# Moving steps of the first block between engines' queues: weight halves, rope-row transposes, a convolution and a gate scan

## The reference, cut to what matters

```python
hx = modulate(rmsnorm(x, norm1_w), sh1, sc1)
hc = modulate(rmsnorm(ctx, norm1_w), csh1, csc1)
aq, ak, av, mq, mk, mv, mo, gates = split(h @ w_in)       # for hx and for hc
aq, ak = rope(rmsnorm(aq)), rope(rmsnorm(ak))             # "rows" below
mq, mk = split(silu(short_conv(concat([mq, mk], -1), conv_qk)))
att = latent_attention(aq, ak, av, cak, cav, sink)        # 4 blocks of 128 queries x 8 heads = 32 units
...
b = jnp.cumsum(lf, -1)                                    # gates, per chunk of 128 tokens
m_t = jnp.maximum(inter, d.max(-1))
```

## Time and profile before

| | |
|---|---|
| median of 3 runs | 2391.23 us (2391.07 to 2391.9) |
| the profiled execution | 2391.57 us |
| its span | 2389.7 us |
| PE busy | 2251.6 us, 94% |
| DVE busy | 1234.8 us, 52% |
| ACT busy | 852.1 us, 36% |
| POOL busy | 363.9 us, 15% |

### The profile page before, as it was taken

The page is one execution under the profiler, slowest core; times in us unless marked ns, Lnnn a source line. Parts: engine busy times, 40 slices in busy tenths (PEclk is TensorE's granted clock), DMA queues, the critical chain, the costliest instruction groups (busy, mean ns, idle before and its releaser), DMA issues.

```text
span 2389.7 us, 28697 instructions
## 1 busy us (share of the span) xinstructions
PE 2251.6 (94%) x11081; PEld 1709.2 (72%) x11081; DVE 1234.8 (52%) x2315; ACT 852.1 (36%) x1498; POOL 363.9 (15%) x273
## 2 busy tenths in 40 slices
PE   7898988779879999999999999999999999999999
PEld 4685677655424676777888888886767788888887
DVE  4643455642102686667654434448776755543442
ACT  4433442432100445544342313334464334322231
POOL 0110123000000454432000000025533200000000
PEclk9999999999999999999999999999999999999999
DMA  8115410258999322221223333232222212333322
GB/s 297 56 46 197 139 36 11 97 186 321 363 387 337 100 71 71 62 79 54 80 89 98 97 97 97 90 92 71 81 61 71 71 58 84 106 99 97 97 87 80
DMA packets 198285, 281.48 MB, mean 118 GB/s; under 512 B 13278, under 2 KB 125448, under 8 KB 198152
## 3 DMA queue, kind: packets, MB, share of 16 engines
q1 hardware_dynamic: 197584, 278.47, 35.0%
q10 hardware_dynamic: 568, 1.19, 0.1%
HBM read 277.52 MB, written 2.10 MB: 117 GB/s over the span
## 4 chain that ended last, share of the span: by engine, by line
PE 76%; DVE 12%; DMA 5%; ACT 4%; issue 2%; SPq 1%; POOL 0%; DVEq 0%; ACTq 0%
PE PS L643 20%; PE PS L645 19%; PE PS L644 19%; PE PS L1401 3%; PE PS L2360 3%; PE PS L2400 2%; PE PS L1383 2%; DMA RX<-in_w_up_dram 1%; PE PS L2267 1%; DVE AL L846 1%; DMA RAW<-in_w_up_dram 1%; PE PS L1393 1%; PE PS L2416 1%; DVE AL L825 1%; DVE AL L838 1%
## 5 line engine op out<-in xcount | busy, mean ns | idle before, releaser
L643 PE MATMUL PS<-OPH,WHI 128*128 128x512 f32 x1224 | 498.3, 407 | 8.2 <-DVE OPL L1440 3.1
L645 PE MATMUL PS<-OPH,WLO 128*128 128x512 f32 x1224 | 481.5, 393 | 0.0
L644 PE MATMUL PS<-OPL,WHI 128*128 128x512 f32 x1224 | 480.5, 393 | 0.0
L594 ACT ACTIVATE WHI<-RAW 128x1024 fp32r<-128x1024 f32 (+2 forms) x286 | 295.5, 1037 | 470.7 <-PE PS L645 461.8
L631 POOL TENSOR_TENSOR WLO<-RAW,WHI 128x1024 fp32r<-128x1024 f32 (+1 forms) x107 | 255.8, 2394 | 1326.8 <-ACT WHI L594 1323.4
L615 DVE TENSOR_TENSOR WLO<-RAW,WHI 128x1024 fp32r<-128x1024 f32 x179 | 214.4, 1200 | 378.4 <-ACT WHI L594 378.4
L643 PEld LDWEIGHTS PS<-OPH,WHI 128*128 128x128 f32 x1224 | 231.9, 189 | 74.5 <-issue 22.5
L645 PEld LDWEIGHTS PS<-OPH,WLO 128*128 128x128 f32 x1224 | 231.8, 189 | 50.0
L644 PEld LDWEIGHTS PS<-OPL,WHI 128*128 128x128 f32 x1224 | 232.3, 190 | 43.6 <-issue 1.0
L643 PE MATMUL PS<-WHI,OPH 128*128 128x512 f32 (+2 forms) x576 | 231.4, 402 | 8.9 <-ACT AL L780 3.8
L645 PE MATMUL PS<-WHI,OPL 128*128 128x512 f32 (+2 forms) x576 | 218.0, 378 | 0.0
(11 more groups left out here) (431 smaller groups left out, 3283.6 us busy)
## 6 DMA issues: line engine op xcount, KB each, us to landing
RAW<-in_w_in_dram SPq DMA_DIRECT2D x102, 512.0 KB, 3.6
RAW<-in_w_ffn_in_dram SPq DMA_DIRECT2D x88, 512.0 KB, 3.5
RX<-in_w_gate_dram SPq DMA_DIRECT2D x42, 512.0 KB, 7.2
RX<-in_w_down_dram SPq DMA_DIRECT2D x42, 512.0 KB, 11.4
RAW<-in_w_ffn_out_dram SPq DMA_DIRECT2D x40, 512.0 KB, 3.4
RAW<-in_w_mod_dram SPq DMA_DIRECT2D x36, 512.0 KB, 4.5
RX<-in_w_up_dram SPq DMA_DIRECT2D x32, 512.0 KB, 10.0
RAW<-in_w_up_dram SPq DMA_DIRECT2D x25, 512.0 KB, 9.2
```

The lines of the kernel that those rows point to most:

```text
L594: hi.up(A.e.activation(q.fhi, q.flat, ACT.Copy), ("w", q.i))
L643: T.e.matmul(o, a[0], b[0], start=first, stop=False)
L644: T.e.matmul(o, a[0], b[1], start=False, stop=False)
L645: return T.e.matmul(o, a[1], b[0], start=False, stop=last)
```

## The change

1. Two pieces' halves (mv's third and fourth) are made between the rope steps of the q rows, on ScalarE and VectorE, in place of behind them.
2. Rows 0 and 1 are turned after mv's third piece, rows 2 and 3 after kv's first; the counter of banks is set back by two so that mk uses the same banks as before.
3. In the attention stage ScalarE's first part of the convolution stands ahead of a weight half (and of the wait for its load) in the same step, its SiLU one step later; VectorE's parts of the convolution are done at steps 7, 9, 15, 16 in place of 6, 8, 14, 16.
4. In steps 32 to 35 VectorE does no step of the gate scan; what is left follows the loop.

```diff
@@ -1180,6 +1180,10 @@
+        def turned0(n):
+            return (0, 0, 2, 2)[n]
@@ pe_proj1
-                    lambda n: pe_rope_turns(min(2 * n, 4)))
+                    lambda n: pe_rope_turns(turned0(n)))
             pe_rows("kv", J["kv"], lhs1, range(6), 256, nothing,
-                    lambda t: [(row_a, (rope_no["kv", t], "q")), (copy_a, ("va", t))], lambda t: None)
+                    lambda t: [(row_a, (rope_no["kv", t], "q")), (copy_a, ("va", t))], lambda t: None,
+                    lambda n: pe_rope_turns(4 if n == 0 else 0))
+            B.i -= 2
@@ act_proj1 (dve_proj1 likewise, with dve_lo and rope_copies(V, "v", ...))
                 if t:
                     act_rope_root(r - 1)
+                if t in (1, 2):
+                    act_hi(J["mv"][t + 1] + 1)
             act_rope_root(3)
             for n, i in enumerate(J["mv"]):
-                act_hi(i + 3)
-                rope_copies(A, "a", min(2 * n, 4))
+                if n >= 2:
+                    act_hi(i + 3)
+                rope_copies(A, "a", turned0(n))
...
-            for i in J["kv"]:
+            for n, i in enumerate(J["kv"]):
                 act_hi(i + 3)
+                rope_copies(A, "a", 4 if n == 0 else 0)
@@ act_between1
             for y in range(34):
+                if y in (6, 8, 14, 16):
+                    act_conv("mq", (6, 8, 14, 16).index(y))
                 if y in HALVES1:
...
-                if y in (6, 8, 14, 16):
-                    act_conv("mq", (6, 8, 14, 16).index(y))
-                if y in (9, 17):
-                    for m in (0, 1) if y == 9 else (2, 3):
+                if y in (10, 18):
+                    for m in (0, 1) if y == 10 else (2, 3):
                         act_conv_end("mq", m)
@@ dve_between1
-                if y in (6, 8, 14, 16):
-                    dve_conv("mq", (6, 8, 14, 16).index(y))
+                if y in (7, 9, 15, 16):
+                    dve_conv("mq", (7, 9, 15, 16).index(y))
@@ dve_att1
-                next(gates, None)
+                if s < 32:
+                    next(gates, None)
```

More of the change, by code:

```diff
@@ L1301, in dve_proj1 @@
                     dve_rope_end(r - 1)
+                if t in (1, 2):
+                    dve_lo(J["mv"][t + 1] + 1)
             dve_rope_end(3)
@@ L1305, in dve_proj1 @@
             for n, i in enumerate(J["mv"]):
-                dve_lo(i + 3)
-                rope_copies(V, "v", min(2 * n, 4))
+                if n >= 2:
+                    dve_lo(i + 3)
+                rope_copies(V, "v", turned0(n))
             for t in range(6):
@@ L1312, in dve_proj1 @@
                     copy_v.up(V.e.tensor_copy(dst[:, :, 0:128], ps(PB["mv", t]).rearrange("p (h e) -> p h e", h=4)), ("mv", t))
-            for i in J["kv"]:
+            for n, i in enumerate(J["kv"]):
                 dve_lo(i + 3)
+                rope_copies(V, "v", 4 if n == 0 else 0)
             for t in range(6):
```

## The result

| | before | after |
|---|---|---|
| median | 2390.85 us (10 runs) | 2383.97 us (10 runs, 2373.13 to 2387.59) |
| profiled execution | 2391.57 us | 2387.59 us |
| its span | 2389.7 us | 2385.8 us |
| mean granted clock of its span | 0.985 | 0.981 |

The account below looks back on a forecast made before the run. TensorE was taken as busy nearly everywhere, so only its waits and lower-clock stretches could yield. Terms 9.9 + 4.1 - 0.5 + 5.1 - 1.9 + 0.8 = 17.5 us gave 2373.7 us, range 2368.5 to 2381.

Parts of the forecast that it names:

- Projection: Projection's mv stage: earlier halves and later-turned rows let TensorE go straight on; gain 9.9 us, bounds 8.0 to 10.5.
- Steps 7 and 8: Attention: unit 8's scores stop waiting for the load; a 1.9 us wait replaces 3.03; gain 4.1 us, 1.9 if clock drops.
- Step 10: Attention: the second convolution stands one step nearer to its user; cost 0 to 1.5 us, taken as 0.5.
- Steps 14 to 16: Attention: unit 15's minimum no longer behind the half; new wait 1.8 us; gain 5.1 us, 3.9 if clock drops.
- Step 18: SiLU one step later: VectorE's gate step meets GpSimd's low half, 2.4 us late, less 0.5 saved; loss 1.9 us.
- Rival A: No collision of gate step and GpSimd's low half at step 18: 2.4 us less, 2371.3 us; chance 0.22.
- Gates held back: Attention's end: TensorE gains 2.2 us, waits 3.8 at the next product, slow matmuls lose 1.4; gain 0.8, between 0 and 2.7.
- a reciprocal under a GpSimd product: Attention's end: reciprocal L1628 taken as not caught by GpSimd's half; if caught, that part's gain is 0 instead of 0.8.
- The sum: Whole kernel: the terms give 17.5 us, and the shift passes unchanged through all later work.
- Rival B: Attention: the new 1.8 to 1.9 us waits drop the clock too; up to 5.4 us, 2377 to 2379; chance 0.20.

Follow-up runs that it names:

- e1: Parts 1 and 2 of the change alone, on the kernel before: 2378.59 us, ratio 0.9954.
- e0_after: The changed kernel unchanged, run a second time: 2383.48 us, ratio 0.9971 to the kernel before.
- e17: The changed kernel with VectorE's sum and products of modulation columns and step 18's gate step moved to step 17: 2375.42 us, ratio 0.9943.
- e16: e7 with VectorE's sum and products of modulation columns and step 18's gate step moved to step 17: 2374.01 us, ratio 0.9932.
- e7: The changed kernel with added matmuls in three TensorE waits (steps 8, 16, first product behind the attention): 2377.94 us, ratio 0.9946.
- e10: e7 with the second SiLU back at step 17: 2373.6 us, ratio 0.9931.
- e15: e14 with VectorE's sum and products of modulation columns and step 18's gate step moved to step 17: 2387.12 us, ratio 0.9992.
- e14: The kernel before with added matmuls ahead of unit 8's scores and step 15's transposes: 2394.21 us, ratio 1.001.
- e12: The kernel before with the second SiLU at step 18 in place of 17, nothing else: 2401.5 us, ratio 1.004.
- e3: Part 4 of the change alone (no gate step in steps 32 to 35), on the kernel before: 2397.2 us, ratio 1.0031.
- e9: The changed kernel with the second SiLU back at step 17: 2380.65 us, ratio 0.9962.
- e8: e1 with added matmuls ahead of unit 8's scores and step 15's transposes: 2378.34 us, ratio 0.9951.

## Why the prediction was wrong, step by step

**Projection: right.** 9.9 forecast, 9.8 in both traces of the changed kernel and in e1's. The part seems to bring more where the clock stays up behind the 2.5 us wait that follows (1.6 us in e1's trace), a gain that the forecast did not have.

**Steps 7 and 8: mechanism and wait right, clock half right.** Forecast 4.1, or 1.9 with a drop. Measured at unit 9: 3.7 without a drop (e0_after), 2.4 and 1.0 with one (after, e17). I took the two waits of the earlier trace rows, 1.92 us with no slow matmul behind it and 2.49 with one, for a boundary. It isn't one: two traces with the same 2.08 us wait fall on either side, and behind the very wait of 2.5 us e1's clock stayed up.

**Step 10: right.** 0.5 forecast, 0.5 measured.

**Steps 14 to 16: size of the clock's part.** Forecast 5.1, or 3.9. At unit 17 e0_after has 4.8 and the first trace 3.4; one unit later 3.1 and 0.3, since the clock is low there, in e0_after only from 6 us behind the wait. The worse case I allowed was 1.2 us; it was 4.8. Not all of this is the wait's: e16 has it filled and loses the same 1.7 us from unit 17 to 18 as e0_after, while e7 and e10, filled likewise, lose 0.1 to 0.2. So why the clock falls there is open.

**Step 18: the term that failed.** The forecast saw the meeting, from a margin of 0.35 us, and priced it at 2.4 us less 0.5. The delay is right (step 19's transposes come 8.7 us behind the scores of unit 18 in place of 6.4 to 6.5 in e15 to e17) and the 0.5 is real (12.69 us before, 12.20 in e17). But the clock falls behind the 1.96 us wait, so that units 18 to 21 lose 5.0. The whole costs 6 to 8 us (e17), 4 to 7 (e15 against e14), 3 to 4 (e16 against e7), 10 to 12 (e12). Rival A, no meeting, did not come true, and it set the meeting at 2.4 us, half of the 5.0 that the units lose.

**Gates held back: wrong in sign.** Forecast 0.8, between 0 and 2.7. TensorE does reach the product 2.5 us earlier, in the traces of after, e0_after, e17 and e3 alike, near the upper bound. The wait there is 2.88 and 3.73 us, near the 3.8 forecast. The 1.4 us for slow matmuls behind it were 3.2 (after) and 4.1 (e0_after), and 4.7 in e3; only in e9's trace were they nothing. Twelve slow matmuls, as assumed, lose 2.4 us and not 1.4 by their spacing in e16 (0.43 us apart at the low clock, 0.23 at the high one). The filled wait gave back 6 of the 7 us of e3's median. With the other parts the gates' part costs about 1 us, which is not resolved. What the prediction could not show, a reciprocal under a GpSimd product, the changed kernel has (VectorE, GpSimd):

```profile
338.54 0.20 DVE L1645 RECIPROCAL AC<-AC 128x8 f32<-128x8 f32 x1
```
```profile
338.44 2.37 POOL L631 TENSOR_TENSOR WLO<-RAW,WHI 128x1024 fp32r<-128x1024 f32 x1
```

It lasts the 0.20 us that it lasts alone, so it is not caught, as the prediction took it.

**The sum.** "I let the shift pass through unchanged" failed: of the leads at 372 us, 10.0 and 11.6, the end has 4.0 and 9.4. e1's trace keeps its lead from 353 us to the end (12.8 and 12.9), so a shift can pass through, but it need not. Rival B (the new waits drop the clock too) is what happened, together with the meeting; its 5.4 us were too few. So three steps failed: the price of the meeting at step 18, the clock behind the new waits, above all at the product, and the passing through. In the changed kernel without the meeting the gain is 13.6 us, and with its waits filled 16.2 (by the ratios), against a forecast of 17.5: what was missing is mostly those two. They are not quite added up: the gap is 10 us, e17 closes 6 to 8 of it, and filling 1.4 to 2.6 more.

**Not settled:** why the executions of e8 fall into two groups (it would fit a meeting in half of them, but only one was traced, and it had none), why e15's median is only 2 us below that of before, and why e12, e3 and the first trace of the changed kernel lose 5 to 6.5 us more behind the attention, where their instructions are those of before.

## What to carry to other kernels

Price a new wait of TensorE of about 2 us at its length plus the slow matmuls that may follow, 0 to 5 us here, and give it as a range: a single trace shows one outcome, and the trace of the kernel before is such a single one too. When a step's phase shifts, list VectorE's two-operand instructions near GpSimd's long ones, however small, and keep them apart by the order of VectorE's own queue, not by a margin between two queues. And measure the parts apart: here parts 1 and 2 alone gained more than the whole.

## What the runs showed of the hardware

The clock can fall with next to no wait ahead. In e16, step 17 (TensorE's timeline), nothing waits over 0.2 us in the 7 us up to here, and from 263.7 to 267.1 the granted clock is 0.50, the lower level of 1.2 GHz; what stands ahead of the fall are sixteen 2x2 matmuls and the small ones of a unit:

```profile
262.00 1.14 PE L1078 MATMUL PS<-cst,AR 2*128 2x2 f32 x16
263.30 0.50 PE L643 MATMUL PS<-WHI,OPH 128*128 128x512 f32 x1 [0.16 <-DVE AR L1254]
263.63 0.59 PE L644 MATMUL PS<-WLO,OPH 128*128 128x512 f32 x1
264.02 0.63 PE L645 MATMUL PS<-WHI,OPL 128*128 128x512 f32 x1
```

And a long wait need not bring it down: behind 3.73 us the clock stayed at 1.00 in e9 and was 0.83 in e0_after over the same 114 matmuls.

A VectorE instruction of 128x8 elements, 0.17 us long, can cost a kernel of 2390 us 3 to 12 us if it meets a GpSimd product of 2.4 us.
